# Four-corner chunk stage and an opening by columns, in a kernel of an RWKV-7 and HGRN2 block

## The chip, the cores and the metric

The kernel runs on one core of one Trainium2 chip. The metric is the device time of one execution in microseconds (us), the median of several. A core has five engines with an instruction queue each: TensorE (PE; its weight loads are listed as PEld), VectorE (DVE), ScalarE (ACT), GpSimd (POOL) and SyncE (SP), the last of which issues the transfers. They wait for one another on semaphores.

## The reference, cut to what matters

The program computes two blocks on x, 512 tokens by 1024 channels, fp32. The change touches two places of the first block, which has two layers. The shift and scale of layer 0 come from a product of the vector c with `w_ada`, and the recurrence of RWKV-7 runs over the tokens in both layers:

```
cond = silu(c) @ w_ada[l] + b_ada[l]              # 1024 x 3072
shift, scale, gate_raw = split(cond, 3)
h = x * (1 + scale) + shift
proj = h @ w_in[l]
...
# per token t, 8 heads of 64 (rwkv7_scan)
sa = einsum('bhvk,bhk->bhv', S, -kk_t)
S  = S * w_t + sa * (kk_t * a_t) + v_t * k_t
y  = einsum('bhvk,bhk->bhv', S, r_t)
```

HGRN2 in the same layers, and a second block with an RG-LRU and a retention layer, are untouched.

## The kernel before

**The chunk stage.** The scan over 512 tokens is done in 8 chunks of 64. For one chunk and one head the recurrence is a handful of 64x64 products: the scores of keys and queries, the inverse of a unit triangular matrix, and then the products that carry the state from chunk to chunk. The 8 heads stand as 4 columns of tiles (`QT` = 4) with two heads each, one on partitions 0 to 63 and one on 64 to 127 (`ROWS`). So every product of a chunk is 8 matmuls of 64x64, and two of them, for the upper and the lower rows, use two corners of the array that lie on its diagonal: rows 0 to 63 with columns 0 to 63, and rows 64 to 127 with columns 64 to 127. `halves_of` writes such a product, one chunk at a time.

The inverse of a chunk is grown in five levels k = 0 to 4. A level is z(k), a product of the scores with the grown inverse x(k-1), of which VectorE takes the part that it needs by a masked copy (`levels`), and then x(k) and its transpose xt(k), made from z(k) and xt(k-1). Before the change x(k) and xt(k) of a chunk stand in one PSUM bank side by side and ScalarE copies both at once (`take_both` into `x_both`, 512 columns).

The jobs of a chunk carry these names in the code: `sb` and `sl` (upper and lower scores), `sk` (key scores), `tok` (scaled keys turned to tokens), `vt` (values turned), `z`, `x`, `xt` (level, grown and turned inverse), `rhs`, `u`, `st`, `y` (right side, updates, next state, output). A helper names the PSUM bank of each: banks 0 to 5 are printed as aux0 to aux5, banks 6 and 7 as proj0 and proj1. `job_open` waits until a bank is free, `job_full` signals its result, `job_ready` waits for that on the reading engine, `job_read` frees the bank and `evacuated_job` waits for it.

Chunks go in pairs. While TensorE carries the state through chunks c and c + 1 it grows the inverses of chunks n = c + 2 and n + 1 between those steps. So a layer has an opening (scores and inverses of chunks 0 and 1), three pairs, and a closing (chunks 6 and 7, no inverses left). The order is written out by hand for each engine, in a function `opening`, `pair` and `closing` of each. On VectorE a pair is: masks of the scores (`mask_scores`), `levels` 0, `next_state`, `levels` 1 and 2, `next_state`, `levels` 3, `mask_keys` twice, `levels` 4. The next state is followed at once by its product with the decay at the chunk's end.

**The opening.** c times `w_ada` for layer 0 is done in four quarters of 512 of the first 2048 columns. Row blocks k = 0 to 7 (128 rows of `w_ada`, 512 columns, 256 KB each) come in by 32 transfers into a ring of 12. Of each quarter VectorE multiplies five row blocks (`ADDED`) with their 128 numbers of c and adds them up (`ada_part_step`), and TensorE takes three (`STREAMED`). There the moving operand is the row block, 512 columns, and the weights are 128 copies of c's column (`c_rows`), so that all 128 rows of the result are equal. `condition(q)` adds what VectorE has added up, by a product with ones. VectorE then picks the diagonal of each 128x128 piece with the identity and sums it, which turns the row into columns (`conditioned_quarter`), makes h = x * scale + shift for two channel tiles per quarter (`modulated`) and splits h in a high and a low part, between ScalarE's `high_h` and its own `low`. One projection step k of the first group of blocks is 12 matmuls (4 blocks, three products of high and low parts each), L2363, and needs channel tile k of h. `stream` and `condition` of the later quarters stand between these steps:

```
if l == 0 and k == 0:
    condition(1)
    stream(2)
if l == 0 and k == 2:
    condition(2)
    stream(3)
```

Behind the opening, VectorE's later steps on the groups' results (L1408) free the banks for the next projection blocks (L2344).

## Time and profile before

| | |
|---|---|
| median of 3 runs | 1913.19 us (1912.94 to 1916.48) |
| profiled execution | 1914.83 us, its span in the trace 1913.0 us |
| mean granted clock of TensorE | 0.982 of full speed |
| TensorE busy | 1826.5 us, 95% of the span |
| VectorE busy | 1101.1 us, 58% |
| ScalarE busy | 816.8 us, 43% |
| GpSimd busy | 702.3 us, 37% |
| DMA, mean over the span | 101 GB/s |

The span is the time from the first to the last record of the profiled execution; the device time holds some 1.8 us around it. Busy shares are means over all stages of the program. The granted clock is the share of full speed at which TensorE was let run in a stretch: 1.00 is 2.4 GHz, 0.50 is 1.2 GHz.

### The profile page before, as it was taken

How to read it: one execution, taken by the hardware profiler on the slowest of the kernel's cores; microseconds unless marked ns; L12 is line 12 of the kernel's file. 1: busy time of each engine (PE TensorE's matmuls, PEld its weight loads, DVE VectorE, ACT ScalarE, POOL GpSimd, SP SyncE). 2: the span in 40 equal slices, each digit the busy share in tenths (PEclk: the TensorE clock that was granted, in tenths of full speed). 3: DMA queues.
4: the chain of work that ended last, by engine and by line, in shares of the span. 5: the costliest groups of instructions: out<-in, count | busy, mean ns of one | idle time of the engine just before them, and what ended most of it. 6: DMA issues, size and time to landing. Idle time of an engine off the chain costs nothing.

```text
span 1913.0 us, 35599 instructions
## 1 busy us (share of the span) xinstructions
PE 1826.5 (95%) x14714; PEld 1453.3 (76%) x14714; DVE 1101.1 (58%) x1431; ACT 816.8 (43%) x1173; POOL 702.3 (37%) x488
## 2 busy tenths in 40 slices
PE   7999999999998999999999997899998999999996
PEld 4778877899775877777899784775676888888875
DVE  7775787633455118787633453658845446546454
ACT  2343645533533443755533534345724324323332
POOL 2454433210252435643210251333453435343332
PEclk9998999999998999999999999999998999999998
DMA  9782222200431522222200432322143322222222
GB/s 366 237 258 71 88 95 93 80 26 4 166 99 44 172 83 83 88 94 89 84 26 4 166 99 88 143 67 66 56 143 123 108 60 84 67 78 72 71 99 99
DMA packets 63201, 193.24 MB, mean 101 GB/s; under 512 B 5936, under 2 KB 6192, under 8 KB 62672
## 3 DMA queue, kind: packets, MB, share of 16 engines
q1 hardware_dynamic: 63056, 191.10, 30.3%
q8 instruction: 116, 1.90, 0.4%
q14 instruction: 29, 0.24, 0.0%
HBM read 173.25 MB, written 17.83 MB: 100 GB/s over the span
## 4 chain that ended last, share of the span: by engine, by line
PE 62%; issue 21%; DVE 7%; POOL 7%; ACT 2%; DMA 0%; POOLq 0%; SPq 0%; DVEq 0%; ACTq 0%
PE proj L2344 39%; POOL w_lo_sb L719 6%; PE aux L2363 4%; PE aux L2602 3%; DVE slots_sb L1405 2%; PE proj L2602 1%; PE aux L2517 1%; PE aux L2659 1%; DVE area_sb L1405 1%; PE aux L2656 1%; PE aux L2962 1%; PE aux L2968 1%; PE aux L2374 1%; PE aux L2959 1%; DVE slots_sb L1408 1%
## 5 line engine op out<-in xcount | busy, mean ns | idle before, releaser
L719 POOL TENSOR_TENSOR w_lo_sb<-w_raw_sb,w_hi_sb 128x512 fp32r<-128x512 f32 x462 | 684.6, 1503 | 1033.3 <-ACT w_hi_sb L806 1033.2
L2344 PE MATMUL proj<-act_hi_sb,w_hi_sb 128*128 128x512 f32 x1480 | 604.0, 408 | 14.9 <-POOL w_lo_sb L719 3.4
L2344 PE MATMUL proj<-act_hi_sb,w_lo_sb 128*128 128x512 f32 x1480 | 579.3, 391 | 0.0
L2344 PE MATMUL proj<-act_lo_sb,w_hi_sb 128*128 128x512 f32 x1480 | 578.3, 391 | 0.0
L806 ACT ACTIVATE w_hi_sb<-w_raw_sb 128x1024 fp32r<-128x1024 f32 x231 | 244.5, 1058 | 673.0 <-PE proj L2344 516.2
L2344 PEld LDWEIGHTS proj<-act_hi_sb,w_hi_sb 128*128 128x128 f32 x1480 | 279.1, 189 | 98.3 <-issue 30.6
L2344 PEld LDWEIGHTS proj<-act_lo_sb,w_hi_sb 128*128 128x128 f32 x1480 | 279.4, 189 | 63.0 <-issue 8.9
L2344 PEld LDWEIGHTS proj<-act_hi_sb,w_lo_sb 128*128 128x128 f32 x1480 | 278.9, 188 | 60.1
L2363 PE MATMUL aux<-act_hi_sb,w_hi_sb 128*128 128x512 f32 x336 | 137.7, 410 | 23.3 <-issue 18.2
L1405 DVE TENSOR_TENSOR area_sb<-area_sb 128x256 f32<-128x256 f32 (+1 forms) x180 | 117.7, 698 | 44.4 <-PE aux L2518 28.2
L2363 PE MATMUL aux<-act_lo_sb,w_hi_sb 128*128 128x512 f32 x336 | 133.5, 397 | 0.0
L2363 PE MATMUL aux<-act_hi_sb,w_lo_sb 128*128 128x512 f32 x336 | 133.4, 397 | 0.0
L1405 DVE TENSOR_TENSOR slots_sb<-slots_sb 128x512 f32<-128x512 f32 (+1 forms) x67 | 84.4, 1262 | 42.3 <-ACT slots_sb L1109 22.6
L1405 DVE TENSOR_TENSOR slots_sb<-proj,const_sb 128x512 f32<-128x512 f32 x44 | 30.4, 691 | 118.5 <-PE proj L2344 118.2
L2363 PEld LDWEIGHTS aux<-act_hi_sb,w_hi_sb 128*128 128x128 f32 x336 | 65.0, 193 | 42.6 <-issue 24.5
L1405 DVE TENSOR_TENSOR area_sb<-area_sb,slots_sb 128x512 f32<-128x512 f32 (+1 forms) x90 | 83.5, 946 | 17.8 <-ACT slots_sb L828 11.3
L2363 PEld LDWEIGHTS aux<-act_lo_sb,w_hi_sb 128*128 128x128 f32 x336 | 64.9, 193 | 15.1 <-issue 1.9
L2363 PEld LDWEIGHTS aux<-act_hi_sb,w_lo_sb 128*128 128x128 f32 x336 | 64.6, 192 | 13.9
L2659 PE MATMUL aux<-area_sb 64*64 64x64 f32 x1280 | 71.9, 218 | 0.4 <-issue 0.2
L2602 PE MATMUL aux<-area_sb 64*64 64x64 f32 x1792 | 68.8, 219 | 3.1 <-issue 2.1
L1408 DVE SCALAR_TENSOR_TENSOR slots_sb<-proj,derived_sb,stage_sb 128x512 f32<-128x512 f32 x24 | 18.0, 751 | 93.2 <-ACT stage_sb L876 93.2
L2602 PEld LDWEIGHTS aux<-area_sb 64*64 64x64 f32 x1792 | 63.8, 135 | 4.3 <-issue 2.7
(310 smaller groups left out, 2557.8 us busy)
## 6 DMA issues: line engine op xcount, KB each, us to landing
w_raw_sb<-wall SPq DMA_DIRECT2D x231, 512.0 KB, 3.6
area_sb<-w_ada SPq DMA_DIRECT2D x32, 512.0 KB, 4.5
slots_sb<-w_ada SPq DMA_DIRECT2D x32, 256.0 KB, 6.9
gate_scr<-stage_sb SPq DMA_DIRECT2D x32, 256.0 KB, 2.2
area_sb<-gate_scr SPq DMA_DIRECT2D x8, 1024.0 KB, 9.7
x_scr<-area_sb SPq DMA_DIRECT2D x3, 2048.0 KB, 7.7
area_sb<-x_scr SPq DMA_DIRECT2D x2, 2048.0 KB, 13.5
area_sb<-lru_gates SPq DMA_DIRECT2D x1, 3584.0 KB, 11.7
```

The lines of the kernel that those rows point to most:

```text
L719: nc.gpsimd.tensor_tensor(w_lo[:, b % 2, :, :].rearrange("p k n -> p (k n)")[:, half], w_raw[:, b % 2, half], w_hi[:, b % 2, :, :].rearran ...
L806: A(w_hi[:, b % 2, :, :].rearrange("p k n -> p (k n)"), w_raw[:, b % 2, :], ACT.Copy)\
L1405: return TT(out_ap, a, b, op)
L1408: return STT(out=out_ap, in0=in0, scalar=scalar, in1=in1, op0=op0, op1=op1)
L2344: ins = MM(bank, w[:, s, k, :], a[:, t, :], start=(start and i == 0), stop=(stop and i == len(terms) - 1))
L2363: ins = MM(bank, w[:, s, 4 * (k % 2) + i, :], a[:, t, :], start=(k == 0 and n == 0), stop=(k == len(tiles) - 1 and n == 2))
L2374: return nc.tensor.transpose(dst, src, C("ident"))
L2517: MM(x[0:64, early], a[:, early], b[:, early], start=True, stop=True)
L2602: ins = MM(x[q, columns * j:columns * j + columns], a[q, j, :], b(q, j), start=(i == 0), stop=(i == len(products) - 1))
L2656: MM(x[q, 64 * j:64 * j + 64], xt[q, j, :], z[q, j, :], start=True, stop=True)
L2659: ins = MM(x[q, at:at + 64], z[q, j, :], xt[q, j, :], start=True, stop=True)
L2959: ins = MM(x, r_vtok[:, c, vs], r_scores[:, cols], start=True, stop=(c == 0))
```

## The change

**Chunk stage.** `beside` takes the place of `halves_of`. It takes several products and writes their matmuls in turns, tile by tile. A product of the odd chunk is marked `across`: its weights and moving data stand on rows q, and its result goes to the other half of the output partitions. The diagonal of the even chunk and the other diagonal of the odd one are then next to each other in the queue. Levels 1 to 4, grown 1 to 3, turned 0 and 4, all scores, tokens and values are written so for two chunks at a time. In turned 1 to 3 one chunk's product stands beside a step of the state's chain. Level 0 and grown 0 stay two-corner products, as do the right side, the updates, the state and the output where they stand alone.

The grown inverse x and the turned one xt have jobs and banks of their own (x with z in banks 0 and 1, xt in banks 2 and 3) and buffers of their own (`x_next`, `xt_next`). ScalarE copies x of the even chunk and xt of both, VectorE x of the odd chunk, 256 columns each. Masks of the lower scores (`mask_lower`) and the product with the chunk end's decay (`end_state`) are moved away from the masks of the upper scores and the next state. The odd chunk's right side and output are added up in PSUM from products of different corners, so a later one waits on a semaphore of the first (`rhs_state`, `y_old`). Scores of the pair after next stand now at the end of a pair, not at its head. The closing steps are written in another order.

TensorE's queue at a turned inverse of the first pair, before (aux2 is the even chunk's bank, aux3 the odd one's; L2656 is the grown half, L2659 the turned one, and x2 are the two corners):

```order
L2656 MATMUL aux2<-area_sb 64x64 x2
L2659 MATMUL aux2<-area_sb 64x64 x2
L2656 MATMUL aux3<-area_sb 64x64 x2
L2659 MATMUL aux3<-area_sb 64x64 x2
L2656 MATMUL aux3<-area_sb 64x64 x2
L2659 MATMUL aux3<-area_sb 64x64 x2
```

And after, the last rows of turned 0 (aux2, aux3) and the first of level 1 (aux0, aux1), at the same place:

```order
L2656 MATMUL aux3<-area_sb 64x64
L2656 MATMUL aux2<-area_sb 64x64
L2656 MATMUL aux3<-area_sb 64x64
L2656 MATMUL aux0<-area_sb 64x64
L2656 MATMUL aux1<-area_sb 64x64
L2656 MATMUL aux0<-area_sb 64x64
```

Before, all matmuls of the even chunk stood ahead of the odd one's; now their banks alternate with every matmul.

VectorE's queue at the end of the first pair, before: next state and its decay, level 3 of both chunks, the two key masks, level 4.

```order
L1405 TENSOR_TENSOR area_sb<-area_sb,proj0 128x256
L1405 TENSOR_TENSOR area_sb<-area_sb,chunk_end_sb 128x256
L1763 COPY_PREDICATED area_sb<-const_sb,aux0 128x256
L1763 COPY_PREDICATED area_sb<-const_sb,aux1 128x256
L1405 TENSOR_TENSOR area_sb<-aux4,const_sb 128x512
L1405 TENSOR_TENSOR area_sb<-aux5,const_sb 128x512
L1763 COPY_PREDICATED area_sb<-const_sb,aux0 128x256
L1763 COPY_PREDICATED area_sb<-const_sb,aux1 128x256
```

And after: the odd chunk's copy of grown 3 (L1808), the next state, two key masks, the decay, the two masks of the lower scores of the coming pair, and level 4.

```order
L1808 COPY area_sb<-aux1 128x256
L1417 TENSOR_TENSOR area_sb<-area_sb,proj1 128x256
L1417 TENSOR_TENSOR area_sb<-aux4,const_sb 128x512
L1417 TENSOR_TENSOR area_sb<-aux5,const_sb 128x512
L1417 TENSOR_TENSOR area_sb<-area_sb,chunk_end_sb 128x256
L1782 COPY_PREDICATED area_sb<-const_sb,aux4 128x256
L1782 COPY_PREDICATED area_sb<-const_sb,proj1 128x256
L1782 COPY_PREDICATED area_sb<-const_sb,aux0 128x256
L1782 COPY_PREDICATED area_sb<-const_sb,aux1 128x256
```

Two key masks, the decay and two lower masks are now between the copy of grown 3 and level 4, where two key masks were between level 3 and level 4.

**Opening.** A row block on TensorE is now four matmuls of one moving column: weights are 128x128 pieces of the `w_ada` rows, the moving column is c's. The result stands as columns at once, so picking and summing are gone, as are the copies of c. VectorE takes 5, 5, 6 and 6 row blocks of the four quarters, TensorE 3, 3, 2 and 2. The modulation of layer 0 is ScalarE's (`modulated`, released by `cond_ready`). `stream` and `condition` have other places between the projection steps, and two chains of small set-up steps (`forget_bounds`, `unit_rates`) stand between VectorE's row blocks.

TensorE's first rows before, up to the first projection matmul (L2400 a streamed row block, L2406 a condition, L2363 the projection):

```order
L2400 MATMUL aux4<-slots_sb,area_sb 128x512 x3
L2406 MATMUL aux4<-slots_sb,const_sb 128x512
L2400 MATMUL aux5<-slots_sb,area_sb 128x512 x3
L2406 MATMUL aux5<-slots_sb,const_sb 128x512
L2400 MATMUL aux4<-slots_sb,area_sb 128x512 x3
L2363 MATMUL aux0<-act_hi_sb,w_hi_sb 128x512
```

And after (L2446 streamed, four matmuls to a row block, L2455 a condition, L2408 the projection):

```order
L2446 MATMUL aux4<-derived_sb,slots_sb 128x1 x12
L2455 MATMUL aux4<-const_sb,slots_sb 128x1 x4
L2446 MATMUL aux5<-derived_sb,slots_sb 128x1 x12
L2408 MATMUL aux0<-act_hi_sb,w_hi_sb 128x512
L2408 MATMUL aux0<-act_lo_sb,w_hi_sb 128x512
L2408 MATMUL aux0<-act_hi_sb,w_lo_sb 128x512
```

Condition 1 (the L2406 on aux5) and stream 2 (the second L2400 on aux4) no longer stand ahead of the first projection matmul; they follow behind 12 and 24 of them.

The diff, cut to its core:

```
-ADDED, STREAMED = (0, 1, 3, 5, 6), (2, 4, 7)
+ADDED = ((0, 1, 3, 5, 6), (0, 1, 3, 5, 6), (0, 1, 2, 3, 5, 6), (0, 1, 2, 3, 5, 6))
...
 ScalarE
+                def modulated(m):
+                    n = SPLITS["h", 0]
+                    if m > 1:
+                        act.wait_ge(split_lo, n + m - 1)
+                    act.wait_ge(S(f"x_first{m}"), 16)
+                    act.wait_ge(S("cond_ready"), m // 2 + 1)
+                    A(ST[m % 2], xa[:, m, :], ACT.Identity, scale=cond[:, 0, 8 + m:9 + m],
+                      bias=cond[:, 0, m:m + 1]).then_inc(split_src, 1)
...
                 def grown(n, k):
+                    take(x_next[0], ("x", l, n, k), 256)
+
+                def turned_inverse(n, k):
                     for e in range(2):
-                        if k < 4:
-                            take_both(x_both[e], ("x", l, n + e, k))
-                        else:
-                            take(xt_last[e], ("x", l, n + e, k))
+                        take(xt_next[e] if k < 4 else xt_last[e], ("xt", l, n + e, k))
...
 VectorE
+                def grown(n, k):
+                    x = heads(job_ready(dve, ("x", l, n + 1, k))[:, 256:512], 64)
+                    job_read(nc.vector.tensor_copy(x_next[1], x), ("x", l, n + 1, k))
...
                 def pair(i):
                     n, c = 2 * i + 2, 2 * i
-                    mask_scores(n)
-                    mask_scores(n + 1)
                     levels(n, 0)
+                    grown(n, 0)
+                    levels(n, 1)
+                    grown(n, 1)
                     next_state(c)
-                    levels(n, 1)
                     levels(n, 2)
+                    grown(n, 2)
+                    end_state(c)
+                    levels(n, 3)
+                    grown(n, 3)
                     next_state(c + 1)
-                    levels(n, 3)
                     mask_keys(n)
                     mask_keys(n + 1)
+                    end_state(c + 1)
+                    if n + 2 < RW_CHUNKS:
+                        mask_lower(n + 2)
+                        mask_lower(n + 3)
                     levels(n, 4)
+                    if n + 2 < RW_CHUNKS:
+                        mask_scores(n + 2)
+                        mask_scores(n + 3)
...
 TensorE
-                        MM(x, c_rows[:, i, :], ada_part[:, n % 12], start=(i == 0), stop=False)                            .then_inc(S("ada_streamed"), 1)
+                        for j in range(4):
+                            ins = MM(x[:, j:j + 1], ada_part[:, n % 12, P * j:P * j + P], DV["c"][:, k:k + 1],
+                                     start=(i == 0 and j == 0), stop=False)
+                        ins.then_inc(S("ada_streamed"), 1)
...
-                def halves_of(name, columns, *products):
-                    x = job_open(pe, name)
+                def beside(*parts):
                     for j in range(QT):
-                        for i, (a, b) in enumerate(products):
-                            for q in ROWS:
-                                ins = MM(x[q, columns * j:columns * j + columns], a[q, j, :], b(q, j),
-                                         start=(i == 0), stop=(i == len(products) - 1))
-                    job_full(ins, name)
+                        for q in range(2):
+                            last = []
+                            for x, across, a, b, start, stop in parts:
+                                n = x.shape[1] // QT
+                                to = ROWS[1 - q if across else q]
+                                last.append(MM(x[to, n * j:n * j + n], a[ROWS[q], j, :], b(ROWS[q], j),
+                                               start=start and (stop or j == 0), stop=stop and (start or j == QT - 1)))
+                    return last
...
                 def pair(i):
                     n, c = 2 * i + 2, 2 * i
-                    chunk_scores(n)
-                    chunk_scores(n + 1)
+                    inverse_level(n, 0)
                     right_side(c)
-                    start_inverse(n)
+                    grow(n, 0)
                     chunk_updates(c)
-                    grow(n, 0)
+                    turn_inverse(n, 0)
+                    inverse_level(n, 1)
                     state_step(c)
-                    inverse_level(n, 1)
+                    grow(n, 1)
+
+                    signalled(beside(turned_part(n, 1, 1)), ("xt", l, n + 1, 1))
+                    evacuated_job(pe, ("st", l, c))
+                    right = half_bank(("rhs", l, c + 1))
+                    last = beside(turned_part(n, 1, 0), (right, True, *state_side(c + 1), True, False))
...
                     inverse_level(n, 4)
-                    for e in range(2):
-                        tokens(n + e)
-                        values(n + e)
-                    grow(n, 4)
+                    if n + 2 < RW_CHUNKS:
+                        upper_scores(n + 2)
+                    tokens(n)
+                    turn_inverse(n, 4)
+                    values(n)
```

## Rows read from the trace of the kernel before

**Rows 1.** Windows: from:to, us, busy (count) of PE PEld DVE ACT POOL, clock, DMA
```profile
371.20:393.90 22.70, 22.10 (x640) 20.89 (x642) 10.21 (x21) 11.74 (x19) 6.69 (x7) 1.00 0.18 61
...
422.97:452.24 29.27, 28.51 (x902) 28.11 (x900) 9.64 (x23) 9.61 (x20) 1.24 (x2) 1.00 0.02 4
...
479.40:489.40 10.00, 7.54 (x230) 6.94 (x226) 0.42 (x1) 2.79 (x8) 0.00 (x0) 1.00 0.01 3
...
946.60:1064.10 117.50, 113.36 (x3523) 110.87 (x3523) 39.62 (x88) 43.23 (x86) 9.18 (x11) 1.00 0.05 15
```

**Rows 2.** Timeline of TensorE's weight loads: start, us, instruction, count, [idle <-releaser]
```profile
371.24 0.88 PEld L2602 LDWEIGHTS aux<-slots_sb 64*64 64x64 f32 x16 [0.34 <-issue]
...
478.39 1.02 PEld L2659 LDWEIGHTS aux<-area_sb 64*64 64x64 f32 x32
...
479.33 0.20 PEld L2602 LDWEIGHTS aux<-area_sb 64*64 64x64 f32 x4
```

**Rows 3.** Timeline, two products in two column halves of the array
```profile
250.00 0.14 PEld L2517 LDWEIGHTS aux<-area_sb 128*64 128x64 f32 x1
250.00 0.14 PEld L2518 LDWEIGHTS aux<-area_sb 128*64 128x64 f32 x1
250.05 0.22 PE L2517 MATMUL aux<-area_sb 128*64 128x64 f32 x1
...
250.06 0.22 PE L2518 MATMUL aux<-area_sb 128*64 128x64 f32 x1
```

**Rows 4.** Timeline of TensorE, matmuls of 512 columns in row halves, then whole
```profile
90.98 1.13 PE L2451 MATMUL aux<-wa_sb,area_sb 64*128 64x512 f32 x4
...
34.66 2.74 PE L2400 MATMUL aux<-slots_sb,area_sb 128*128 128x512 f32 x6
```

**Rows 5.** Timeline of ScalarE, closing of layer 0
```profile
480.53 0.38 ACT L1037 ACTIVATE area_sb<-aux 128x256 f32<-128x256 f32 x1 [0.55 <-PE aux L2602]
...
481.73 0.38 ACT L1037 ACTIVATE area_sb<-aux 128x256 f32<-128x256 f32 x1 [0.82 <-PE aux L2602]
```

**Rows 6.** Timeline of VectorE, a steady pair
```profile
422.97 0.69 DVE L1405 TENSOR_TENSOR area_sb<-aux,const_sb 128x512 f32<-128x512 f32 x1 [4.74 <-PE aux L2602]
423.58 0.44 DVE L1763 COPY_PREDICATED area_sb<-const_sb,proj 128x256 f32<-128x256 int32 x1
...
429.88 0.42 DVE L1405 TENSOR_TENSOR area_sb<-area_sb,proj 128x256 f32<-128x256 f32 x1 [2.82 <-PE proj L2602]
```

**Rows 7.** Timeline of ScalarE, end of a pair
```profile
421.56 0.85 ACT L1037 ACTIVATE area_sb<-aux 128x256 f32<-128x256 f32 x2
```

**Rows 8.** Timeline of the opening, and of one-column matmuls behind it
```profile
17.92 1.29 DVE L1405 TENSOR_TENSOR act_lo_sb<-stage_sb,act_hi_sb 128x512 fp32r<-128x512 f32 x2 [0.24 <-ACT act_hi_sb L814]
...
18.76 0.30 PEld L2400 LDWEIGHTS aux<-slots_sb,area_sb 128*128 128x128 f32 x2 [1.74 <-DMA slots_sb<-w_ada]
...
27.93 0.80 PE L2363 MATMUL aux<-act_hi_sb,w_hi_sb 128*128 128x512 f32 x1
...
61.83 1.40 DVE L1408 SCALAR_TENSOR_TENSOR slots_sb<-aux,derived_sb,stage_sb 128x512 f32<-128x512 f32 x2
...
67.45 0.47 PE L2344 MATMUL proj<-act_hi_sb,w_hi_sb 128*128 128x512 f32 x1 [1.96 <-DVE wa_sb L1408]
...
157.56 8.39 PEld L2427 LDWEIGHTS aux<-const_sb,area_sb 128*128 128x128 f32 x48
```

**Rows 9.** Windows of the opening's end and of one-column matmuls
```profile
65.00:70.00 5.00, 3.04 (x10) 2.11 (x9) 0.75 (x1) 4.96 (x6) 3.02 (x3) 0.78 0.35 117
...
160.00:170.00 10.00, 10.00 (x34) 7.72 (x34) 9.58 (x18) 0.00 (x0) 2.50 (x2) 0.50 0.32 105
```

**Rows 10.** Chain of waits, one link: start, us, instruction, count
```profile
112.33 22.00 PE proj L2344 x96
```

More of the change, by code:

```diff
@@ L1535, in _ @@
+            conditioned_quarter(3)
+            lows_of(3)
             for l in range(DEPTH):
@@ L2741, in pair @@
+                    key_scores(n)
                     grow(n, 3)
-                    key_scores(n)
-                    key_scores(n + 1)
-                    inverse_level(n, 4)
-                    for e in range(2):
-                        tokens(n + e)
-                        values(n + e)
-                    grow(n, 4)
+                    keyed, own = output_parts(c + 1, out)
+                    after_old(c + 1)
+                    last = beside(turned_part(n, 3, 0), keyed)
+                    job_full(last[0], ("xt", l, n, 3))
```

578 lines of the change are left out of this document (343 added, 235 removed).

## The prediction

> **What bounds the kernel now.** The page's first part has TensorE as its busiest engine by far, but that is an average, so I read the stretches that the change touches, by windows. In the chunk stage of layer 0 (371.2 to 489.4, 118.2 us) and of layer 1 (946.6 to 1064.1, 117.5 us) TensorE is busy nearly without a break at full clock, and VectorE and ScalarE are each busy about a third of the time [rows 1]. A steady pair of chunks takes 29.27 us and holds 902 matmul records [rows 1]; each fp32 matmul leaves two, so it is 448 matmuls (I count them in the code) and some 6 records of the neighbours. So the stage is bound by how fast small matmuls leave TensorE. That rate is in [rows 2]: 16 matmuls of 64x64 (32 records) take 0.94 us from the first weight load to that of the next group. Two of them, on the two corners of the diagonal, share one slot. I call 8 such matmuls a step, S = 0.47 us. Eight matmuls with 128 moving columns take 0.88 us, and some 0.81 without the last load's tail [rows 2].
>
> **The chunk stage: matmul time.** Nothing is removed; 416 small and 32 wide matmuls stay in a steady pair: 52 S + 32/8 x 0.88 = 27.9 us, of the 29.27. Afterwards groups of even and odd chunk are written in turns, the odd one with its output half crossed, so that four corners of the array have work. Four-corner steps hold 16 matmuls. By the new order a steady pair has 18 of them (levels 1 to 4: 4; grown 1 to 3: 3; turned 0 and 4: 2; turned 1 to 3 with a step of the chunk recurrence: 5; lower scores 1; tokens 2; values 1), 16 two-corner steps (level 0 and grown 0: 4; right sides 3; updates 2; state 2; output 3; old output 1; turned 1 of the odd chunk 1) and two wide ones. What does a four-corner step cost? No row shows four corners of 64x64, so I bound it: 2 S if nothing more overlaps, 1 S if all does. Nearest rows: two column halves over all 128 rows, so the whole array, with different operands in each, load weights at 250.00 both and start matmuls at 250.05 and 250.06, 10 ns apart [rows 3]; and two row halves over all 128 columns, 4 records of 512 columns in 1.13 us with the last one's tail, where 6 such records one after the other take 2.74, so 4 some 1.8 [rows 4]. Rows overlap, columns overlap, and the array filled whole starts pairs as close as the diagonal does. I take 1 S. Then the pair has 34 S + 2 x 0.84 = 17.6 us of matmul time.
>
> The Trainium skill (TensorE: Matmul & The Clock Gate, Part 3, "What overlaps and what doesn't") says that a weight load overlaps matmuls in flight only where the row group differs. The new order puts two corners of the same rows next to each other, so by it a four-corner step would be nearer 2 S and the stage would gain nothing. [Rows 3] disagree: the two halves have the same 128 rows, and both loads run at once. It is rival C.
>
> **The chunk stage: waits.** At 17.6 us the hand-overs begin to count, so I walked one steady pair, engine by engine. A link from a step to its reader and back is read in closing: ScalarE's copies start at 480.53 and 481.73, 1.20 apart with one step of 0.47 between [rows 5]: 0.38 for the copy, 0.35 for the ways there and back. VectorE's masked copy takes 0.44, the two of a level 0.88; a mask multiply holds it 0.61 (422.97 to 423.58) [rows 6], two 256-wide copies on ScalarE take 0.85 [rows 7]. VectorE's new copy of the odd chunk's grown inverse I price as its nearest row, 0.42 [rows 6]; it runs beside ScalarE's copy for the even one, 0.38 [rows 5], where ScalarE had two of double width. What lies on the path, in the order of the new pair: (a) after grown 3 VectorE has next state, two key masks, end state and two lower masks in front of level 4 (0.42 + 1.3 + 0.43 + 0.7, then 0.8), so turned 4 waits 0.55; (b) level 0 of the next odd chunk waits for the masks of its upper scores, 0.55; (c) ScalarE has the turned inverses, two token tiles and then the values, so the right side waits 0.5; (d) grown 1 waits for level 1's copies, 0.2; (e) the step with the state side waits for the next state, which VectorE does only behind the copy of grown 1, 0.65. Other links are covered by steps written between. Sum 2.5: the pair takes 20.15. The pair of before has 1.4 beyond its matmul time, of which I can place about 1.0 in waits, so I add the unplaced 0.4: 20.5, or 8.7 us less, though the first pair has 2 S less than a steady one, before and after, and the last one no new scores after.
>
> By stretch, per layer: opening to the first right side 22.7 + 2.7 (the two chunks' scores that headed pair 0) = 25.4 before; now 22.5, since VectorE's normalisation and key masks (2.9 us) stand before level 1 and TensorE waits 2.2 there. The three pairs: 118.2 - 25.4 - 10.0 = 82.8 before [rows 1]; now 19.2 + 20.15 + 19.45 + 3 x 0.4 = 60.0. Closing: 10.0 before [rows 1], a chain of links; the key and old-state products now stand inside the waits, 8.5. Layer 0: 118.2 - 91.0 = 27.2. Layer 1, 117.5 before: 26.5. What comes behind waits for the last chunk output, so it all moves up. **Term 1: -53.7.**
>
> **The opening.** Before, TensorE's first projection matmul starts at 27.93, behind condition 1 and stream 2, though its input was ready at 19.2 (17.92 + 1.29) [rows 8]. Now only stream 0, condition 0 and stream 1 stand before it. The last row of stream 1 lands at 18.76 [rows 8]. A one-column matmul has no row in the opening; the nearest, 48 records with 128x128 weights in 8.39 us [rows 8], gives 0.17 a record, 1.4 us for a row of w_ada (0.9 and 1.7 are the ends, for the streamed 512 columns of before). So the first k step starts at 20.3. It runs at 1.2 GHz, since one-column matmuls did not hold the clock up either: 0.50 in 160 to 170 [rows 9]. A k step is 12 matmuls at 0.229 (22.00/96 [rows 10]), 2.7 us. With conditions at 1.0, streams of two rows at 1.6, and 3.3 us from a condition to its first h (0.3 on VectorE, then two modulations and splits on ScalarE, then a subtraction), the steps end at 25.0, 28.8, 33.0, 36.8, 41.1, 44.8, 48.1 and 50.9, against 54.1 before (27.93 + 96 x 0.227 + 5 x 0.86, the five streamed or condition matmuls between): -3.2. DMA is busy all the while and does not get faster, but weights and rows come in time for these steps. Next, VectorE reaches the first rw groups at 61.83, behind its five later steps, and TensorE waits for the proj bank until 67.45, 1.96 us, and then runs at 0.78 in that window [rows 8, 9]. VectorE sheds four picks, four reductions and eight modulations and gets two more rows of w_ada: enough to be out of the way, worth the 1.96 and up to 1.3 of clock. Ends: 0, if a wait on DMA comes in place of both, and -6.5. **Term 2: -5.5.**
>
> **Sum.** The profiled execution took 1914.8, its span 1913.0; the median is 1913.2, 1.6 lower. 1914.8 - 53.7 - 5.5 = 1855.6, as a median **1854 us**.
>
> **The rivals.**
> A, as above: 1854, 0.80. Its own range: 1.2 us per pair, 3 per layer at the ends, 3 in the opening: 1840 to 1868.
> B, TensorE cannot start work that fast, and a four-corner step costs 1.5 S. For it: in these rows no stretch has more than one record per 29 ns (0.94/32 [rows 2]). Against: neighbours start 10 ns apart [rows 3], so a start by itself is not that long. 18 x 0.23 = 4.2 a pair, of which 1.5 goes into waits: +2.7 x 6 and +2 at the ends, 1872. Chance 0.09. The Trainium skill (same page, "Wait — 56ns, not 53.3ns?") has a floor of about 25 ns between matmul starts however few the columns; an estimate from that figure is 32 x 25 = 0.80 us for a four-corner step, 1.7 S. The 10 ns of [rows 3] speak against it as a floor between different parts of the array; of the average nothing here tells.
> C, no overlap beyond two: the pair keeps 27.9 and its waits, term 1 falls to 0 +- 3, only the opening is left: 1908. Chance 0.07.
> D, the slow side: the waits of (a) to (e) or the 2.2 us in the opening let TensorE's clock fall to 1.2 GHz in the chunk stage. 17.6 becomes 35.2 a pair, 5.9 more than before, with the ends +46: 1953. It decides from half the stage at the low level. For it: a wait of 1.96 us came with 0.78 [rows 8, 9]. Against: closing has TensorE busy 7.54 of 10 us at 1.00 [rows 1]. Chance 0.04.
>
> **Range and chances.** 0.2% is about what a measurement of this kernel can tell from no change. 1836 to 1882 holds A and most of B, A widened since a walk misses waits. Faster by over 0.2%: A, B and half of C, 0.92; within it 0.03; slower 0.05.
>
> **What will show it.** A four-corner group with two outputs in turns: 32 records in some 0.47 us if A, 0.94 if C. The steady pair, from one mask multiply of the upper scores to the next: 20.5. The granted clock 1.00 in both stages. First projection matmul at 20 to 21, no wait of 2 us near 60. I am wrong if VectorE's queue (the copies at the end of a pair) holds TensorE by over 4 us a pair, or if a one-column stretch drags the clock of the k steps.

## The result, and the profile after

The changed kernel takes 1900.92 us (median of 4 runs, 1899.03 to 1902.64); the kernel before, run beside it, 1913.07 (1911.55 to 1916.48). The ratio is 0.9926, 95% interval 0.9912 to 0.9941: 11 to 17 us faster. The prediction was 1854 with a range of 1836 to 1882. The direction was right, the size was not, and the time lies outside the range.

I read the places of [rows 1 and 8] again. First the timeline of TensorE in the opening, then at the first level of the inverse:

```profile
21.12 0.77 PE L2408 MATMUL aux<-act_hi_sb,w_hi_sb 128*128 128x512 f32 x1
...
366.50 0.29 PE L2656 MATMUL aux<-slots_sb 64*64 64x128 f32 x1 [0.18 <-issue]
...
374.21 1.16 PE L2656 MATMUL aux<-area_sb 64*64 64x64 f32 x64 [1.27 <-DVE area_sb L1420]
```

The first projection matmul starts at 21.12 (before 27.93 [rows 8]) and the chunk stage of layer 0 at 366.50 (before 371.24 [rows 2]). The last row is the core of the matter: 64 records, that is turned 0 and level 1 of two chunks, two four-corner steps, in 1.16 us with the tail of the last one. A four-corner step costs what a two-corner step cost, some 0.47. Now the windows of the stage (columns as in [rows 1]), between the same mask multiplies of the upper scores:

```profile
366.50:389.47 22.97, 16.60 (x674) 14.72 (x674) 12.00 (x28) 10.80 (x22) 6.68 (x7) 1.00 0.19 61
389.47:413.42 23.95, 17.76 (x789) 16.66 (x793) 10.80 (x27) 7.25 (x20) 0.00 (x0) 1.00 0.02 4
413.42:440.50 27.08, 20.09 (x899) 18.93 (x888) 10.83 (x28) 8.66 (x24) 1.20 (x2) 1.00 0.02 4
440.50:472.00 31.50, 21.28 (x961) 19.94 (x961) 10.19 (x24) 10.85 (x30) 1.20 (x2) 1.00 0.02 5
472.00:482.50 10.50, 9.40 (x223) 8.30 (x221) 0.42 (x1) 2.30 (x6) 0.00 (x0) 0.84 0.02 3
```

The steady pair (413.42 to 440.50) takes 27.08 us, not the 20.5 of the prediction; before it took 29.27 [rows 1]. TensorE is busy 20.09 of it, where it was busy 28.51. It stands still for 7 us, and these are pauses of its weight loads in that window:

```profile
415.58 0.13 PEld L2656 LDWEIGHTS proj<-wa_sb,slots_sb 64*64 64x64 f32 x1 [1.95 <-issue]
419.32 0.31 PEld L2656 LDWEIGHTS aux<-area_sb 64*64 64x64 f32 x6 [1.34 <-issue]
423.05 0.48 PEld L2656 LDWEIGHTS aux<-area_sb 64*64 64x64 f32 x25 [0.49 <-issue]
424.81 1.05 PEld L2656 LDWEIGHTS aux<-area_sb 64*64 64x64 f32 x48 [0.38 <-issue]
...
430.58 0.26 PEld L2656 LDWEIGHTS aux<-area_sb 64*64 64x64 f32 x12 [0.80 <-issue]
434.28 0.13 PEld L2656 LDWEIGHTS proj<-area_sb 64*64 64x64 f32 x1 [1.28 <-issue]
```

None of these ends with a semaphore of another engine: the releaser is "issue" (the row left out is the one other pause, 0.57 us for VectorE, ending at 426.42). And all but the short one at 424.81 end 3.7 us apart, or twice that: 415.58, 419.32, 423.05, and 430.58, 434.28. The waits over all pairs of the layer (389.47 to 472.00: who waited for whom, us in total, times, longest):

```profile
PE aux L2656 <- issue: 10.3, 14, 1.6
PE proj L2656 <- issue: 9.4, 7, 1.8
PE proj L2656 <- ACT area_sb L1033: 1.6, 1, 1.6
PE aux L2656 <- DVE area_sb L1417: 1.2, 2, 0.7
```

19.7 us are "issue"; in the pairs of before (393.90 to 479.40) it was 0.5. Where the 12.1 us between the two profiled spans came from: 4.8 by the start of the first stage, 3.1 in that stage (119.4 us from its first matmul to the first group-norm step of VectorE, now 116.3), 4.2 in the stage of layer 1 (118.6, now 114.3), nothing elsewhere.

These parts are those of one pair of executions. The traces of the kernels below show how far they wander. The changed kernel profiled once more (r1_after) starts its first stage at 368.84 and takes 119.6 and 115.6 us for the two; with the stage's part of the change alone (f3_stage_only) they take 113.1 and 116.7. With the old order all six readings lie between 118.4 and 119.4 (before, e4_before_padded, f2_opening_only). So the stage's gain is real, but a single trace tells it to some 3 us at best.

**Theories.** 1, supply: TensorE's instructions come in pieces of 16 KB (the instruction queue moves 7 of them, 0.11 MB, in the 27.08 us), and a new one comes every 3.5 to 4 us at best. An fp32 matmul leaves two weight loads and two matmul records. If each of the four is an instruction of 64 bytes, a piece holds 64 matmuls (128 matmul records). 64 matmuls on two corners take 3.75 us, just as long; on four corners 1.9 us, and then TensorE waits. 2, hand-overs: the pauses are waits for VectorE and ScalarE under a wrong label. 3, the array cannot keep four corners at work for long.

### The profile page after: what moved, and what is told of

It is laid out like the page before. It is cut to its first block, busy times and chain, and to the rows that moved or that the text cites. A ratio compares the mean times of both kernels' runs of the same rounds, so it can differ in the third digit from the quotient of the medians.

```text
span 1900.9 us, 35878 instructions
## 1 busy us (share of the span) xinstructions
PE 1766.7 (93%) x14794; PEld 1397.0 (73%) x14794; DVE 1101.9 (58%) x1446; ACT 815.6 (43%) x1213; POOL 702.1 (37%) x488
## 4 chain that ended last, share of the span: by engine, by line
PE 64%; issue 15%; DVE 12%; ACT 4%; POOL 3%; DMA 1%; SPq 0%; POOLq 0%; DVEq 0%; ACTq 0%
PE proj L2389 42%; PE aux L2408 5%; PE aux L2656 4%; DVE area_sb L1417 3%; POOL w_lo_sb L708 3%; DVE slots_sb L1420 3%; DVE slots_sb L1417 2%; PE aux L2569 1%; PE proj L2656 1%; PE aux L3140 1%; PE aux L3146 1%; PE aux L2419 1%; DVE slots_sb L2079 1%; PE aux L2430 1%; PE aux L3137 1%
## 5 line engine op out<-in xcount | busy, mean ns | idle before, releaser
L2408 PE MATMUL aux<-act_hi_sb,w_hi_sb 128*128 128x512 f32 x336 | 138.4, 412 | 25.6 <-issue 18.2
L2656 PE MATMUL aux<-area_sb 64*64 64x64 f32 x4096 | 110.7, 222 | 33.2 <-issue 20.4
L2408 PE MATMUL aux<-act_lo_sb,w_hi_sb 128*128 128x512 f32 x336 | 134.7, 401 | 0.0
L2408 PE MATMUL aux<-act_hi_sb,w_lo_sb 128*128 128x512 f32 x336 | 134.3, 400 | 0.0
L2656 PEld LDWEIGHTS aux<-area_sb 64*64 64x64 f32 x4096 | 99.7, 135 | 44.0 <-issue 34.4
L1417 DVE TENSOR_TENSOR slots_sb<-slots_sb 128x512 f32<-128x512 f32 (+1 forms) x67 | 85.6, 1280 | 42.9 <-ACT slots_sb L1121 22.5
L1033 ACT ACTIVATE area_sb<-aux 128x256 f32<-128x256 f32 x136 | 50.0, 384 | 124.4 <-PE aux L2656 121.6
L2408 PEld LDWEIGHTS aux<-act_hi_sb,w_hi_sb 128*128 128x128 f32 x336 | 65.4, 195 | 45.0 <-issue 25.3
L2408 PEld LDWEIGHTS aux<-act_lo_sb,w_hi_sb 128*128 128x128 f32 x336 | 65.4, 195 | 14.5 <-issue 1.2
L2408 PEld LDWEIGHTS aux<-act_hi_sb,w_lo_sb 128*128 128x128 f32 x336 | 65.4, 195 | 14.2
```

Of the source, the lines that this page charges most:

```text
L1033: job_read(A(dst, heads(x[:, at:at + 256], 64), ACT.Copy), job)
L1417: return TT(out_ap, a, b, op)
L2408: ins = MM(bank, w[:, s, 4 * (k % 2) + i, :], a[:, t, :], start=(k == 0 and n == 0), stop=(k == len(tiles) - 1 and n == 2))
L2656: last.append(MM(x[to, n * j:n * j + n], a[ROWS[q], j, :], b(ROWS[q], j), start=start and (stop or j == 0), stop=stop and (start or j == Q ...
```

## The experiments

**Bursts without any wait** (e1_bursts), behind the stage of layer 0:

```
+                if l == 0:
+                    rest(2)
+                    burst(320, 4)
+                    rest(3)
+                    burst(320, 2)
...
+                            MM(aux[bank][ROWS[1 - q if across else q], at:at + wide], C("unit")[ROWS[q]],
+                               P1[ROWS[q], i % 4, 0:wide], start=True, stop=True)
```

> The changed kernel with bursts of 64x64 fp32 matmuls added behind the chunk stage of layer 0, which wait for nothing and whose results nobody reads: 320 in turns on four corners, 320 on the two corners of the diagonal, 256 on four corners with 128 moving columns, 256 on four corners with one satisfied wait ahead of each, 160 on the whole array with 64 columns, and 12 wide matmuls between the bursts. Theory 1, supply of instructions: TensorE's instructions come in pieces of 16 KB, one every 3.6 to 3.7 us at best, and a piece holds 64 matmuls (7 pieces came in the steady pair of 450). Then the first burst runs at 29 ns a matmul for one or two pieces' worth and then waits with 'issue' at 58 a matmul: 320 take 14 to 18 us, not 9.4. Two corners take 18.7 us with hardly a stall. 128 columns on four corners take 56 ns each, 14.5 us, nearly no stall, so twice the work per instruction is free. With a wait ahead of each the piece holds fewer matmuls: 72 ns each in the long run, 15 to 18 us for 256. Rival 2, the waits in the stage are for VectorE and ScalarE and are only labelled issue: the first burst takes 9.4 us, the fourth about the same per matmul plus some 7 ns each. Rival 3, the array cannot keep four corners at work: the first burst slows evenly, without gaps, and 128 columns slow down as much.

Timeline of TensorE in that kernel: the four-corner burst, the two-corner burst, four corners with 128 columns:

```profile
503.97 3.16 PE L2958 MATMUL aux<-slots_sb,const_sb 64*64 64x64 f32 x128 [4.23 <-issue]
507.70 2.24 PE L2958 MATMUL aux<-slots_sb,const_sb 64*64 64x64 f32 x128 [0.57 <-issue]
511.70 2.10 PE L2958 MATMUL aux<-slots_sb,const_sb 64*64 64x64 f32 x128 [1.76 <-issue]
515.71 1.28 PE L2958 MATMUL aux<-slots_sb,const_sb 64*64 64x64 f32 x72 [1.91 <-issue]
...
527.41 18.88 PE L2958 MATMUL aux<-slots_sb,const_sb 64*64 64x64 f32 x640
...
556.72 14.20 PE L2958 MATMUL aux<-slots_sb,const_sb 64*64 64x128 f32 x512
```

This has no hand-over in it, and the pauses are there: exactly 128 records and then a pause, with 3.7 to 4.0 us from one start to the next. Within a piece the records are 15 ns apart (2.10 us with the tail), except in the first one behind the long pause, 3.16 us, where the granted clock was 0.61. The burst takes 20.2 us for 320 matmuls (496.83 to 516.99); on two corners the same number takes 18.88 without a pause. So theory 2 cannot be the cause of such pauses, and theory 3 falls too, since the records within a piece come back to their 15 ns. Four corners with 128 columns go through without a pause, 55 ns a matmul, twice the work of the two-corner burst's 59 ns. The fourth burst, with a satisfied wait ahead of each matmul, again paused every 128 records: 256 matmuls in 13.2 us, 51 ns each with the pieces that stood ready, not the 72 that I expected. So one wait adds nothing that a piece counts.

**Without the crossing** (e2_no_cross):

```
-                                to = ROWS[1 - q if across else q]
+                                to = ROWS[q]
```

> The changed kernel, with the crossing taken out: same order, same instructions and same waits, but every product stays on the two corners of its rows, as before the change. Theory 1, supply: a matmul now costs 58 ns in the array, just what its instructions cost to bring, so a steady pair goes from 27.1 to 28 to 30 us and the kernel loses 4 to 16 us: 1905 to 1917. Rival 2, waits for other engines: 18 four-corner steps a pair cost 0.47 more each, 8.5 us a pair, of which at most the 5.5 us of gaps labelled issue can absorb some: +3 to +8.5 a pair and +2 to 4 at the ends, 1923 to 1960.

1923.28 us, ratio to before 1.0036 (1.0023 to 1.0048). That is 6 us beyond what theory 1 allowed and just inside rival 2's band, so by the total my expectation failed. The windows say why. A steady pair takes 29.26 us (423.61 to 452.87), no more "issue" than before, and equal to the 29.27 of before: within the 28 to 30 expected.

```profile
423.61:452.87 29.26, 28.48 (x902) 28.13 (x900) 10.94 (x26) 8.67 (x24) 1.20 (x2) 1.00 0.02 4
```

What I had left out are the opening and the closing of the stage: from its first matmul to the first group-norm step it is 124.4 and 124.6 us for the two stages, 5 and 6 more than before. So the new order by itself costs 5 to 6 us a stage, and the crossing gives 5 to 10 back (counted against both profiled executions of the changed kernel, the measured one and r1_after). In a steady pair it gives 2.2 of the 8.5 that 18 overlapped steps are worth.

**Half of the tiles left out** (e3_half_tiles):

```
-                    for j in range(QT):
+                    for j in range(2):
                         for q in range(2):
                             last = []
```

> The changed kernel with half of the chunk stage's matmuls left out (two of the four columns of tiles), all hand-overs and all copies of VectorE and ScalarE kept at full size. Theory 1, supply: half the instructions, so a steady pair falls from 27.1 to what hand-overs cost plus half of the array time, 14 to 18 us, and the gaps labelled issue vanish: both stages together give 55 to 75 us back, total 1825 to 1845. Rival 2, waits for other engines: only array time goes, 17.6 / 2 = 8.8 a pair at most, pair 18.3 to 20, gaps labelled issue of the same length stay: total 1845 to 1865.

The other two of the four columns of tiles are never computed. One run: 1842.29 us, 17.67 a steady pair (405.14 to 422.81). Waits of TensorE from 388.14 to 440.00:

```profile
PE aux L2656 <- DVE area_sb L1782: 5.0, 9, 0.8
PE aux L2656 <- DVE area_sb L1417: 3.4, 4, 1.0
PE proj L2656 <- DVE area_sb L1782: 2.8, 4, 1.1
PE proj L2656 <- issue: 1.1, 1, 1.1
PE aux L2656 <- issue: 1.0, 4, 0.3
```

With half the instructions "issue" all but vanishes, and now VectorE's masked copies are what TensorE waits for. The pair is 9.4 us shorter, more than the 8.8 that rival 2 allowed as array time, though the clock was at 0.90 in that window. Both the pair and the total are in theory 1's band, each near the edge towards rival 2's. And the instruction queue moves 14 pieces in the stage where it moves 28 with all tiles.

**More instructions for the same work**, on the kernel before (e4_before_padded, f4_before_padded2):

```
                             for q in ROWS:
+                                pe.wait_ge(S("const_in"), 16)
+                                pe.wait_ge(S("c_spread"), 3)      # the second only in f4
                                 ins = MM(x[q, columns * j:columns * j + columns], a[q, j, :], b(q, j),
```

> The kernel before the change, with one satisfied wait added ahead of each small matmul of the chunk stage (some 1630 per layer): no more work, only more instructions. Theory 1, supply: the kernel before stands just at the supply's rate (58.7 ns a matmul in the array, 57 to bring its instructions), so with a quarter more instructions a steady pair goes from 29.3 to 32 to 33.5 us, the two stages together +18 to +35 us. Rival 2: the queue runs ahead of the array, and some 7 ns for a wait hide behind 58 ns of matmul: 0 to +3 us.

> The kernel before the change with two satisfied waits ahead of each small matmul of the chunk stage. With one wait nothing happened (+2.1 us): the matmul's own instruction carries it, and the same 26 or 27 pieces came. With two, an instruction of its own is needed. Theory 1, supply: 33 to 34 pieces come per stage instead of 27, a steady pair goes from 29.3 to 32 to 35 us, the kernel takes 20 to 45 us longer. Rival: the waits go through beside the array's work, pieces increase but time does not, 0 to +5.

e4: one run of 1918.13 us, 2 above the median of before beside it (1916.03, runs from 1913.24 to 1917.95), with 28 pieces in the stage as before: nothing was added that a piece counts, so it tests nothing. f4: 2166.6 us, 252 more, far beyond either theory. The instruction queue's rows for the stage of layer 0, before (371.27 to 490.63) and f4 (373.91 to 616.53):

```profile
q8 instruction: 28, 0.46, 1.6%
q8 instruction: 34, 0.56, 0.9%
```

Both stages have the same 3525 matmul records, so the 6 pieces more are the added waits: 6 x 16 KB over some 1630 matmuls is 60 bytes for each, an estimate that fits one instruction of 64. A piece therefore counts instructions or bytes and not matmul records. But the pieces came mostly 6 to 8 us apart, so the supply was not what held f4: a matmul with a second wait simply takes long. The next bursts price it. (The granted clock was 0.82 in that stage, which may be part of the 252.)

**Longer rests, padded and single-pass bursts** (f1_bursts), with `rest(2, 60)` ahead of the bursts, two waits ahead of each matmul in one, and `act_hi` as operand of the fp32r one.

> Bursts behind the chunk stage of layer 0 again, nobody reads their results; wide matmuls of 0.43 us per record stand between them so that the supply can fill up: 60 wide, 640 four-corner fp32 matmuls; 30 wide, 192 on one corner; 60 wide, 512 four-corner ones with two satisfied waits ahead of each, which no longer fit into the matmul's own instruction; then 60 wide and 1536 matmuls of 64x64 in the single-pass fp32r form, on two row halves in turns. In the first bursts 12 wide matmuls gave 1.45 to 1.9 pieces before the first gap, and five transfers of 16 KB came one behind the other in the next pause. Theory 1, supply: after 60 wide matmuls some 4 to 6 pieces are waiting, so the first 250 to 400 four-corner matmuls run at 15 ns a record with no gap, and then a gap comes every 64 matmuls, one piece per 3.7 to 4.0 us. One corner: array time alone, 117 ns a matmul, no gap. Two waits each: one more 64-byte instruction per matmul, 51 matmuls in a piece, 75 to 80 ns each in the long run. fp32r: two instructions instead of four, so 128 matmuls in a piece, 31 ns each in the long run if the array is faster than that. Rival, the limit is on starts or on matmul records whatever their instructions: the padded burst keeps 64 matmuls per gap and 62 ns, the fp32r burst has 62 ns as well (64 per 4 us) or no gaps.

```profile
534.50 3.38 PE L2961 MATMUL aux<-slots_sb,const_sb 64*64 64x64 f32 x216
538.95 2.09 PE L2961 MATMUL aux<-slots_sb,const_sb 64*64 64x64 f32 x128 [1.07 <-issue]
542.67 2.09 PE L2961 MATMUL aux<-slots_sb,const_sb 64*64 64x64 f32 x128 [1.63 <-issue]
546.13 2.10 PE L2961 MATMUL aux<-slots_sb,const_sb 64*64 64x64 f32 x128 [1.36 <-issue]
...
668.60 68.47 PE L2961 MATMUL aux<-slots_sb,const_sb 64*64 64x64 f32 x1024
843.63 44.99 PE L2958 MATMUL aux<-act_hi_sb 64*64 64x64 f32 x1536
```

After 50 us of wide matmuls (60 of them leave 120 records of 0.43 us) only 216 records (1.7 pieces) were ready, not 4 to 6. Then again 128 records per pause, 3.46 us from start to start five times, 3.72 twice and 4.00 once. One corner took 22.61/192 = 118 ns a matmul without a pause, as expected: with 59 on two corners and 29 on four inside a piece, the corners run side by side at no loss. With two waits a matmul takes 68.47/512 = 134 ns, not the 75 to 80 expected, and there is no pause: the second wait costs 105 ns beside the 29 of a four-corner matmul. The fp32r burst took 29.3 ns a matmul and did not pause, so it is no slower than the supply of 128 in 3.75 us, which leaves open whether the supply or the array set it.

The instruction queue in that trace, one column per us from 530 to 570:

```profile
GB/s 0 0 0 0 0 0 16 0 0 0 16 0 0 16 0 0 0 16 0 0 16 0 0 0 16 0 0 16 0 0 0 16 0 0 0 16 0 0 0 16
q8 instruction: 10, 0.16, 1.6%
```

Ten transfers of 16 KB, one to a piece: from the second on (540) each begins 1.0 to 1.6 us behind the start of a piece (538.95, 542.67, 546.13 and so on), takes some 1 us, and the next piece starts 1.2 to 1.6 us after it has landed. In e1 they follow the starts in the same way. I had read five of e1's as a store being filled in one pause; they belong to the pieces of the burst (501.36, 505.09, 509.07, 513.39 and 517.16), and the store of my expectation for f1 is not there.

**16-bit words** (g1_half_words):

```
+                        MM(aux[i % 2 if corners == 4 else 0][ROWS[1 - q if across else q], ...],
+                           C("unit")[ROWS[q]].bitcast(mybir.dt.bfloat16)[:, 0:64],
+                           C("unit")[ROWS[q]].bitcast(mybir.dt.bfloat16)[:, 64:128], start=True, stop=True)
```

> Two bursts of 1280 matmuls of 64x64 in 16-bit words behind the chunk stage of layer 0 of the changed kernel, the first on four corners, the second on the two of the diagonal; nobody reads the results. Such a matmul leaves one record and takes two instructions, where one in fp32 leaves two records and takes four. Theory 1, supply of 16 KB per 3.5 to 4.0 us: 128 of them in a piece, gaps every 128 matmuls, 27 to 31 ns each in the long run, 1280 in 35 to 40 us, on four corners and on two alike if two corners need less than that. Rival, the limit counts matmuls whatever their instructions: 64 per 3.5 to 4.0 us, 70 to 80 us. Rival, it counts nothing but starts, at 15 ns a record: 19 us and no gaps.

```profile
551.37 1.92 PE L2966 MATMUL aux<-const_sb 64*64 64x64 bf16 x128 [1.53 <-issue]
554.82 1.92 PE L2966 MATMUL aux<-const_sb 64*64 64x64 bf16 x128 [1.53 <-issue]
558.28 1.92 PE L2966 MATMUL aux<-const_sb 64*64 64x64 bf16 x128 [1.53 <-issue]
```

128 matmuls with one record each and then a pause, 3.45 us apart (3.73 for the first ones): 1280 took 33.5 us on four corners, a little under the 35 to 40 expected, and 34.8 on two. The limit does not count matmuls. It counts what a matmul leaves: 128 matmul records and their 128 weight loads, whether these are 64 matmuls or 128. The window of the four-corner burst says one thing more:

```profile
551.37:567.00 15.63, 9.50 (x640) 8.94 (x640) 0.00 (x0) 0.00 (x0) 0.00 (x0) 0.50 0.02 5
```

The granted clock was 0.50, so the array ran at half speed, and the pieces came just as fast as at 1.00 in f1 (3.46). What sets their pace is not TensorE's array. That TensorE reads them from outside at a limited rate is the reading that fits all of this; what happens between a transfer and the next start was not looked into.

**The two parts of the change apart** (f2_opening_only, f3_stage_only): the hunks on `ADDED`, `c_rows`, the row blocks' waits, `modulated`, `conditioned_quarter`, `stream`, `condition` and `conditioning` in the one, the job plan, `beside` and the `opening`, `pair` and `closing` of all engines in the other.

> The kernel before with the opening's part of the change alone (one-column matmuls, 5, 5, 6, 6 row blocks, modulation on ScalarE, the other order of conditions). The chunk stage began 4.77 us earlier in the changed kernel. If the two parts are independent: 4.0 to 5.5 us faster than before, 1908 on a chip where before takes 1913 (ratio 0.9975). Rival, the opening's gain is taken up by the larger stage behind it or depends on it: ratio 1.000.

> The kernel before with the chunk stage's part of the change alone. In the traces the two stages are 3.1 and 4.3 us shorter: ratio 0.996, 6.5 to 8.5 us faster than before. Rival: if the stage gains by starting with a fuller store of instructions or by the clock that the new opening leaves, it gives 0 to 4.

f2: ratio 0.9952 (0.9936 to 0.9969), 6 to 12 us faster, more than the 4.0 to 5.5 expected; f3: 0.9962 (0.9946 to 0.9978), 4 to 10, as expected. The sum of both, 16.5, is more than the 14 of the whole, but within the intervals. So the opening is worth about as much as the four-corner stage. Where f2 gained its time no trace shows: its profiled execution was the slowest of the four (1914.36), with the stage starting at 370.29, 1.0 before that of the kernel before.

**Three kernels beside each other** (r1_after, h6_copies_on_scalar, h5_pairs). h6 gives the odd chunks' copies back to ScalarE:

```
                 def grown(n, k):
-                    take(x_next[0], ("x", l, n, k), 256)
+                    for e in range(2):
+                        take(x_next[e], ("x", l, n + e, k), 256)
```

h5 replaces two 64-column weights by one of 128 in tokens and values, for which GpSimd puts the two chunks side by side beforehand:

```
+                def turned_pair(x, at, t):
+                    for j in range(QT):
+                        last = [MM(x[q][:, at + 64 * j:at + 64 * j + 64], t[ROWS[q], j, :], C("unit")[ROWS[q]],
+                                   start=True, stop=True) for q in range(2)]
+                    return last
```

> The changed kernel again, as the yardstick for the kernels that are built on it and run on the same chip: 0.9926 of the kernel before, as measured.

> The changed kernel, with the odd chunks' grown inverses copied by ScalarE behind those of the even ones, not by VectorE. Theory 1, supply: the extra 0.38 us in the chain of each level falls into gaps in which TensorE has no instructions anyway: 0 to +4 us over the changed kernel. Rival, hand-overs: four copies of 0.38 a pair later, 1.5 a pair and as much in the opening, +10 to +13 us in all.

> The changed kernel with fewer instructions for the same products: the turned tokens and values of an even and an odd chunk come from one matmul with 128 weight columns (64 rows, output to all partitions) instead of two with 64. GpSimd puts the two chunks side by side beforehand (scaled keys into buffers that were free, values in place). 96 of some 1760 small matmuls of a stage go, the array's time does not: half as many matmuls, each of which takes up twice the columns. Theory 1, supply: 1.5 pieces fewer per stage at 3.6 to 3.9 us, 5.5 a stage where the supply is the limit all the way, so 5 to 11 us less than the changed kernel: ratio to the kernel before 0.987 to 0.990. Rival, the limit lies in the array or in hand-overs to VectorE and ScalarE: 0, or 2 to 6 slower, since GpSimd's work (some 5 us a pair) is now in the chain.

Ratios to the kernel before: r1 0.9919 (0.9901 to 0.9936), h6 0.9933 (0.9919 to 0.9948), h5 0.9927 (0.9908 to 0.9946). h6 is 1.5 us over r1 by the medians, inside theory 1's 0 to 4 and far from the rival's 10: which engine copies the odd inverse hardly matters while TensorE waits for instructions. h5 gained nothing, where theory 1 had 5 to 11 us for it; the result is the rival's 0. Its steady pair took 26.91 us. The stage had 26 pieces, not 28, and "issue" in the first stage was 15.7 us (21.7 in the measured kernel, 24.1 in r1), but the array's time rose by as much:

```profile
442.66 0.27 PE L2721 MATMUL proj<-const_sb,wa_sb 64*128 64x64 f32 x1
442.67 0.27 PE L2721 MATMUL aux<-const_sb,wa_sb 64*128 64x64 f32 x1
442.78 0.27 PE L2721 MATMUL proj<-const_sb,wa_sb 64*128 64x64 f32 x1
442.78 0.27 PE L2721 MATMUL aux<-const_sb,wa_sb 64*128 64x64 f32 x1
```

In either bank a record comes every 0.11 us, and a matmul leaves two: two matmuls side by side take 220 ns, 110 each, where one with 64 weight columns takes 29 on four corners. 24 of them replace 48 in a pair: +1.2 us of array time (24 x 110 - 48 x 29 ns), against 0.375 pieces less, -1.4 us. So theory 1 had the pieces right and left the array's price out. The granted clock also fell, to 0.50 from 444 to 450 and 0.84 over 442.69 to 475.00, so what this trade is worth at full clock stays open, but it is small.

## Why the prediction was wrong

**What bounds the kernel now** was half right. [Rows 1 and 2] show small matmuls leaving TensorE at 58.6 ns each, and I took that for the only limit. It is the array's rate, but also, by chance, the rate at which their instructions come: 64 in 3.75 us from the array, one piece in 3.5 to 4.0 us from the supply. Two limits lay on top of each other, and the change removed one.

**A four-corner step takes 1 S**: right, shown in the stage (64 records in 1.16 us) and in the bursts (15 ns a record). So rival C fell: corners of the same rows load and run at once. "17.6 us of matmul time" for a pair goes with the 20.09 of busy time measured, which holds the tail of every group as well. The rule behind rival C (the Trainium skill, TensorE: Matmul & The Clock Gate, Part 3, "What overlaps and what doesn't": a weight load overlaps matmuls in flight only where the row group differs) does not hold in these runs. The floor of about 25 ns between starts (the Trainium skill, same page, "Wait — 56ns, not 53.3ns?") is not one here either, with records 15 ns apart on different corners.

**The step that failed is the one behind it**, "The chunk stage: waits", where the pair is put together as 17.6 us of matmul time plus 2.5 of hand-overs plus 0.4. A floor was missing: 450 matmuls are 7.03 pieces, at 3.46 to 4.0 us 24 to 28 us, whatever the array does. Measured: 27.08, or 3.85 a piece. The three pairs of layer 0 took 82.5 us where my walk had 60.0, which is 22.5 of the 24 us by which the layer missed its 27.2. The hand-overs I walked are real, but they mostly fall beside the supply's pauses: e3 shows them once the supply no longer binds. Its pair took 17.67, where 2.9 of hand-overs and 8.8 of array would be 11.7. Of the 6.0 beyond that, 1.6 are waits (TensorE is idle for 4.5 us of the pair) and 4.4 are busy time (13.15 us), at a granted clock of 0.90. So my walk missed waits too, but steps of half the length also cover less of a hand-over, and whether this order would reach 20.5 with unlimited supply was not measured.

**Term 1** was -53.7; the two stages gave -3.1 and -4.2 (r1_after: +0.2 and -2.9). **Rival B** (TensorE cannot start work that fast) had the right shape and the wrong cause. It argued from starts, and priced a four-corner step at 1.5 S with 1872 as the result. The limit is no price per start, it is a rate over a whole piece, and no step-by-step sum shows it. What I could have seen in the trace of before: the recorded transfers of the instruction queue, one 16 KB piece about every 4 us all through the stage, at the very pace of the array.

**Term 2** was -5.5; the trace gives -4.8 at the start of the stage and f2 -6 to -12. The size is near, but in part by luck. The first projection matmul is at 21.12 (said: 20 to 21). The k steps, though, should have ended at 50.9 and gained 3.2 us; the next group of projections starts at 55.00, where before it started at 54.45:

```profile
42.54 0.63 PE L2408 MATMUL aux<-act_hi_sb,w_hi_sb 128*128 128x512 f32 x1
...
49.44 0.47 PE L2408 MATMUL aux<-act_hi_sb,w_hi_sb 128*128 128x512 f32 x1 [0.48 <-DVE act_lo_sb L1417]
...
55.00 0.39 PE L2389 MATMUL proj<-act_hi_sb,w_hi_sb 128*128 128x512 f32 x1
```

So 6.8 us of head start were gone by the end of the k steps. Waits for VectorE took 1.6 of it (none in that stretch of before), and from 42 to 45 the granted clock was 0.50, with matmuls 0.43 us apart instead of 0.23. One of my signs of being wrong, a clock that drags the k steps, did show. The first 8 projection matmuls were 0.43 apart too, as I had assumed for 1.2 GHz, though the window lists 1.00 there. The other half of the term came and was larger: the wait of 1.96 us and the low clock behind it are gone, and the 96 projection matmuls from there take 21.8 us (55.00 to 76.76), before 25.6 (54.45 to 80.01). That is 3.8, where the term had 3.3; the last 1.6 of the 4.8 fell between 150 and 175 us, and I did not trace why. It is no fixed gain either: the stage starts at 366.5 to 370.3 in the ten traces with the new opening and at 368.9 to 373.9 in the four with the old one.

**Rival D** did not come in the measured kernel. The granted clock stayed at 1.00 through the pairs, though TensorE stood idle for a quarter of them. Only the closing fell to 0.84, and took 10.5 us, not 8.5. In kernels near it the clock did fall for a while inside the stage: h5 (0.50 from 444 to 450), f3 (0.89 from 440.9 to 452.9), h6 (0.87 from 380 to 393).

## What to carry to other kernels

Before you let more small matmuls run side by side, count the instructions, not only the array's time: 64 fp32 matmuls (or 128 that leave one record each, as bf16 did) per 3.5 to 4.0 us was all that TensorE got here, so below 54 to 62 ns per fp32 matmul nothing is gained beyond the one or two pieces that stand ready. More moving columns per matmul do help (128 columns on four corners: 55 ns, no pause); more weight columns do not (110 ns). A pause with the releaser "issue" that comes back at even distances after the same number of records is the sign of it, and the transfers of the instruction queue, one to each pause, confirm it. Take a rate that looks like an engine's limit in a trace as an upper bound, and ask what else has that rate.

## What the runs showed of the hardware that I had not expected

- Pieces of 128 matmul records, 3.46 to 4.0 us from one to the next, and 1.4 to 1.9 pieces ready at the start of a burst, whether TensorE had been at wide matmuls for 10 us (e1) or for 50 (f1). The pace is the same at a granted clock of 0.50 and of 1.00 (g1, f1).
- The recorded instruction transfers (16 KB, 0.9 to 1.3 us each in f1) come 3.3 to 4.0 us apart in such a stretch, one to a piece, each beginning 1.0 to 1.6 us after TensorE started on a piece. The trace of before has 28 of them in the stage of layer 0, 3.9 us apart in the median, though nothing waits for them there.
- A first satisfied wait on each small matmul cost nothing that e1 or e4 could tell; a second one raised a matmul from 29 ns to 134 in the burst of f1.
- Two fp32 matmuls of 64 rows and 128 weight columns, side by side on different rows, take 220 ns with 64 moving columns; one on the whole array takes 224 (e1: 160 in 35.8 us). Four of 64x64 take 117.
